# Two-layer hybrid backbone, attention stage: value halves side by side, neighbour bias added by TensorE, normaliser divided out by GpSimd

## The reference

```python
s = jnp.einsum('bqhd,bkhd->bhqk', q, k).astype(jnp.float32) * scale
p = jax.nn.softmax(s, axis=-1).astype(v.dtype)
return jnp.einsum('bhqk,bkhd->bqhd', p, v)
# B, latent queries: 8x16 window on a grid 64 wide, learned bias, then all context keys
s_loc = jnp.einsum('bwhd,brwkhd->bhwrk', qr, kn).astype(jnp.float32) * NA_SCALE
s_loc = (s_loc + bias.astype(jnp.float32)).reshape(B, H, GRID_W, kr * kc)
p = jax.nn.softmax(jnp.concatenate([s_loc, s_ctx], axis=-1), axis=-1).astype(v.dtype)
```

## Time and profile before

| | us |
|---|---|
| median of 3 runs | 3155.1 (3154.56 to 3157.39) |
| the profiled execution, its own time | 3152.75 |
| its span, first to last instruction | 3151.2 |
| TensorE busy (matmuls) | 3005.9 (95%) |
| VectorE busy | 1641.4 (52%) |
| ACT busy | 917.2 (29%) |
| GpSimd busy | 223.2 (7%) |

### The profile page before, as it was taken

The page is one execution under the profiler, slowest core; times in us unless marked ns, Lnnn a source line. Parts: engine busy times, 40 slices in busy tenths (PEclk is TensorE's granted clock), DMA queues, the critical chain, the costliest instruction groups (busy, mean ns, idle before and its releaser), DMA issues. The chain is left out here.

```text
span 3151.2 us, 44954 instructions
## 1 busy us (share of the span) xinstructions
PE 3005.9 (95%) x17054; PEld 2608.0 (83%) x17054; DVE 1641.4 (52%) x2910; ACT 917.2 (29%) x1433; POOL 223.2 (7%) x252
## 2 busy tenths in 40 slices
PE   7999999989988899999999899999998989999999
PEld 3888888878978787888888788888876979778887
DVE  4664466444466736652664566255244467643333
ACT  2221122123366522211222222112222367432221
POOL 1300000021213100000000000000002123000000
PEclk9999999999999999999999999999999999999999
DMA  7543243212100023332432234233212200223332
GB/s 240 124 126 100 80 126 106 81 53 56 44 13 1 26 61 104 112 112 65 127 116 85 67 113 134 59 111 100 72 50 67 66 12 7 67 80 106 88 96 91
DMA packets 412202, 263.55 MB, mean 84 GB/s; under 512 B 11700, under 2 KB 403672, under 8 KB 412088
## 3 DMA queue, kind: packets, MB, share of 16 engines
q1 hardware_dynamic: 407256, 253.14, 26.9%
q0 software_dynamic: 2752, 4.66, 0.9%
q10 hardware_dynamic: 2080, 4.19, 0.4%
HBM read 256.13 MB, written 6.68 MB: 83 GB/s over the span
## 5 line engine op out<-in xcount | busy, mean ns | idle before, releaser
L406 PE MATMUL pair<-h_hi,w_hi 128*128 128x512 f32 x2912 | 1029.9, 354 | 46.9 <-DVE h_lo L529 23.2
L407 PE MATMUL pair<-h_lo,w_hi 128*128 128x512 f32 x2912 | 963.4, 349 | 0.0
L410 PE MATMUL pair<-h_hi,w_lo 128*128 128x512 f32 x2912 | 819.9, 350 | 0.0
L406 PEld LDWEIGHTS pair<-h_hi,w_hi 128*128 128x128 f32 x2912 | 555.3, 191 | 181.6 <-issue 46.5
L407 PEld LDWEIGHTS pair<-h_lo,w_hi 128*128 128x128 f32 x2912 | 555.5, 191 | 73.3
L380 DVE TENSOR_TENSOR w_lo<-w_raw,w_hi 128x1024 fp32r<-128x1024 f32 (+1 forms) x276 | 362.7, 1315 | 307.5 <-ACT w_hi L373 301.0
L410 PEld LDWEIGHTS pair<-h_hi,w_lo 128*128 128x128 f32 x2912 | 471.8, 192 | 19.8
L373 ACT ACTIVATE w_hi<-w_raw 128x1024 fp32r<-128x1024 f32 (+1 forms) x276 | 307.8, 1116 | 614.1 <-PE pair L410 589.0
L406 PE MATMUL pair<-s_hi,w_hi 128*128 128x512 f32 x1232 | 426.6, 346 | 0.0
L407 PE MATMUL pair<-s_lo,w_hi 128*128 128x512 f32 x1232 | 400.5, 344 | 0.0
L647 DVE SCALAR_TENSOR_TENSOR mod_acc<-mod_raw,cs,mod_acc 128x256 f32<-128x256 f32 x896 | 365.3, 480 | 0.0
(11 more groups left out here) (215 smaller groups left out, 3390.7 us busy)
## 6 DMA issues: line engine op xcount, KB each, us to landing
mod_raw<-in_w_mod SPq DMA_DIRECT2D x64, 1024.0 KB, 5.0
w_raw<-in_w_ffn_gate SPq DMA_DIRECT2D x88, 512.0 KB, 3.8
w_raw<-in_w_ffn_up SPq DMA_DIRECT2D x88, 512.0 KB, 3.8
w_raw<-in_w_ffn_down SPq DMA_DIRECT2D x64, 704.0 KB, 4.6
w_raw<-in_w_in SPq DMA_DIRECT2D x32, 512.0 KB, 4.0
w_raw<-in_w_out SPq DMA_DIRECT2D x12, 512.0 KB, 4.1
w_raw<-in_w_q_up SPq DMA_DIRECT2D x8, 576.0 KB, 4.1
mod_first<-in_w_mod ACTq DMA_DIRECT2D x2, 2048.0 KB, 12.3
```

Of the source, the lines that this page charges most:

```text
L406: eng.matmul(dst, wh, rh, start=first, stop=False)
L407: eng.matmul(dst, wh, rl, start=False, stop=False)
L410: last = eng.matmul(dst, wl, rh, start=False, stop=end)
```

## The change

Four things change in the attention stage.

Values: `v_hi` and `v_lo` of one head lie side by side in one stationary operand of 128 columns (`v_both`, `vn_both`). One matmul with `p_hi` gives v_hi p_hi in rows 0 to 63 and v_lo p_hi in rows 64 to 127, and a second, of 64 columns, adds v_hi p_lo to the first half. The two halves are added when y is evicted. The values of the neighbour heads are split per pair instead of all at once.

Bias: the tables themselves are split into `na_hi` (ACT) and `na_lo` (VectorE), and TensorE adds them to the scores with two matmuls of a split identity. Maximum and exponential of all chunks read PSUM. `bias_at` gives the steps of the eight splits: 2 and 4 of each layer, 56 and 62 of layer 0, 38 and 42 of layer 1. `na_lo` takes the place of `na_tt` in memory.

Normaliser: ACT copies the spread reciprocals to `inv_sum`, one row buffer, and one half of y to `y_f`; VectorE adds the other half; GpSimd multiplies a whole head pair's y by `inv_sum` once it is complete (`pair_ends`, step 4 of the next pair). What waited for y (`y_hi`, the loads of the output weights) waits for `a_scaled`.

Start: ACT copies the identity to fp32r.

```diff
 TensorE
+    if biased(l, s):
+        eng.wait_ge(bias_lo_done, bias_tables(l, s))
     for a, b in keys:
         eng.matmul(dst, qh[rows, q], kh[rows, a:b], start=True, stop=False)
         eng.matmul(dst, qh[rows, q], kl[rows, a:b], start=False, stop=False)
+        if biased(l, s) and a == 0:
+            for table in (na_hi, na_lo):
+                eng.matmul(dst, ident_r[:, :], table[:, j, first:first + SEQ], start=False, stop=False)
...
+    vals = v_both[:, :, 2 * i + j, :] if kind == "mla" else vn_both[i][:, :, j, :]
-        eng.matmul(dst, vh[:, k, i * P:(i + 1) * P], ph, start=k == kc[0], stop=False)
-        eng.matmul(dst, vh[:, k, i * P:(i + 1) * P], pl, start=False, stop=False)
-        last = eng.matmul(dst, vl[:, k, i * P:(i + 1) * P], ph, start=False, stop=k == kc[-1])
+        if first:
+            eng.matmul(dst, vals[:, k, :], ph, start=True, stop=False)
+        last = eng.matmul(dst[0:V_DIM], vals[:, k, 0:V_DIM], pl, start=False, stop=False)
+        if not first:
+            last = eng.matmul(dst, vals[:, k, :], ph, start=False, stop=end)
 ACT, even step from 6 on, then after the exponential
     eng.wait_ge(a_pv, c0 // 2 + b + 1)
+    wait_if(eng, a_scaled, 6 * l + 2 * b // att_chunks(l))
+    eng.activation(inv_sum[r, q0:q0 + 2 * P], psum2[r, bank + 2 * P:bank + 4 * P], ACT.Copy).then_inc(a_inv, 1)
-    eng.activation(y_f[r, ...], psum2[r, bank:bank + 2 * P], ACT.Copy).then_inc(a_copied, 1)
+    eng.activation(y_f[r, ...], psum2[other, bank:bank + 2 * P], ACT.Copy).then_inc(a_copied, 1)
...
+    if bias_at(l, s):
+        i, j = bias_at(l, s)
+        eng.wait_ge(tt_loaded[j], 16 * (2 * l + i + 1))
+        eng.activation(na_hi[:, j, :], na_tt[:, j, :], ACT.Copy).then_inc(bias_hi_done, 1)
 GpSimd
+    k = pair_ends(l, s)
+    if k is not None:
+        eng.wait_ge(a_out, (ATT_C0[l] + (k + 1) * att_chunks(l)) // 2)
+        eng.tensor_tensor(y_f[:, k, 0:w], y_f[:, k, 0:w], inv_sum[:, 0:w], ALU.mult).then_inc(a_scaled, 1)
 VectorE, step s
     eng.wait_ge(a_s, c0 + s + 1)
-    if not own_scores(l, s):
-        eng.tensor_tensor(prob[:, s % 3, 0:SEQ], pair[s % 2][:, 0:SEQ], na_tt[:, j, first:first + SEQ], ALU.add)
-        eng.tensor_copy(prob[:, s % 3, SEQ:TOK], pair[s % 2][:, SEQ:TOK])
     eng.tensor_reduce(stat[:, s % STATS, 0:1], ..., AX_X, ALU.max, negate=True).then_inc(a_max, 1)
+    if bias_at(l, s):
+        i, j = bias_at(l, s)
+        eng.wait_ge(bias_hi_done, 4 * l + 2 * i + j + 1)
+        eng.tensor_tensor(na_lo[:, j, :], na_tt[:, j, :], na_hi[:, j, :].bitcast(F32), ALU.subtract)\
+           .then_inc(bias_lo_done, 1)
     (reciprocal of chunk s-1)
     (even step: y)
+    eng.wait_ge(a_inv, c0 // 2 + b + 1)
     eng.wait_ge(a_copied, c0 // 2 + b + 1)
-    eng.tensor_tensor(y, y, psum2[r, bank + 2 * P:bank + 4 * P], ALU.mult).then_inc(a_out, 1)
+    eng.tensor_tensor(y, y, psum2[r, bank:bank + 2 * P], ALU.add).then_inc(a_out, 1)
     (pt_lo of chunk s-2)
 SyncE, tables of the second neighbour pair
-    eng.wait_ge(a_max, ATT_C0[l] + 4 * nb + (nb // 2) * (j + 1))
+    eng.wait_ge(a_s, ATT_C0[l] + 4 * nb + (nb // 2) * j + SEQ // P)
```

More of the change, by code:

```diff
@@ L263, in program @@
         vn_f = sb("vn_f", [P, TOK // P, NA_WIDTH], F32, "sarea", na_at + 4 * TOK * 4)
-        v_hi = sb("v_hi", [P, TOK // P, MLA_HEADS * V_DIM], F32R, "sarea", 0)
-        v_lo = sb("v_lo", [P, TOK // P, MLA_HEADS * V_DIM], F32R, "sarea", 4 * TOK * 4)
+        v_both = sb("v_both", [P, TOK // P, MLA_HEADS, 2 * V_DIM], F32R, "sarea", 0)
         y_f = sb("y_f", [P, 6, TOK], F32, "harea", KD * TOK * 4)
-        vn_hi = sb("vn_hi", [P, TOK // P, NA_WIDTH], F32R, "sarea", 14 * TOK * 4)
-        vn_lo = sb("vn_lo", [P, TOK // P, NA_WIDTH], F32R, "sarea", na_at + 4 * TOK * 4)
+        vn_both = [sb(f"vn_both{i}", [P, TOK // P, 2, 2 * NA_DIM], F32R, at, off * TOK * 4)
+                   for i, (at, off) in enumerate((("harea", 4), ("sarea", 14)))]
         wo_first = sb("wo_first", [P, 2, KD * P], F32, "sarea", 8 * TOK * 4)
@@ L285, in program @@
                                    ("ks_lo1", "wring", 12)))]
+        ident_r = sb("ident_r", [P, P], F32R)
         na_tt = sb("na_tt", [P, 2, BIAS_SLOTS * GRID_W], F32, "scratch", 0)
+        na_lo = sb("na_lo", [P, 2, BIAS_SLOTS * GRID_W], F32R, "scratch", 0)
+        na_hi = sb("na_hi", [P, 2, BIAS_SLOTS * GRID_W], F32R, "wring", 13 * TOK * 4)
+        inv_sum = sb("inv_sum", [P, TOK], F32, "scratch", 3 * TOK * 4)
         mod_raw = sb("mod_raw", [P, KD, 2 * P], F32)
@@ L350, in program @@
         a_hi, a_lo, v_hi_done = sem("a_hi"), sem("a_lo"), sem("v_hi_done")
-        a_s, a_max, a_exp, a_rsum, a_copied, a_t, a_pth, a_ptl, a_pv, a_out, a_bias = (
-            sem(f"a_{k}") for k in ("s", "max", "exp", "rsum", "copied", "t", "pth", "ptl", "pv", "out", "bias"))
+        a_s, a_max, a_exp, a_rsum, a_copied, a_t, a_pth, a_ptl, a_pv, a_out = (
+            sem(f"a_{k}") for k in ("s", "max", "exp", "rsum", "copied", "t", "pth", "ptl", "pv", "out"))
+        a_inv, a_scaled = sem("a_inv"), sem("a_scaled")
+        bias_hi_done, bias_lo_done, ident_ready = sem("bias_hi_done"), sem("bias_lo_done"), sem("ident_ready")
         a_latent_t, a_latent_hi, a_latent_lo = (sem(f"a_latent_{k}") for k in ("t", "hi", "lo"))
@@ L1168, in mix_act @@
                         eng.wait_ge(c_read, C_READS * l + 3)
-                        eng.activation(token_values(v_hi, t), unit_values(o), ACT.Copy, scale=c_stat[:, 3, t:t + 1])\
+                        eng.activation(token_values(0, t), unit_values(o), ACT.Copy, scale=c_stat[:, 3, t:t + 1])\
                            .then_inc(v_hi_done, 1)
@@ L1485, in program @@
         ATT_C0 = [0, 6 * 12]
-        ATT_SPLITS = 21
+        ATT_SPLITS = 22
         def chunk_info(l, c):
@@ L1517, in splits, with biased, bias_tables, bias_at @@
             i = g - MLA_HEADS
[L1518 to L1523, removed]
-            kind, _, _, q0, _ = chunk_info(l, c)
-            return kind == "mla" or q0 >= SEQ
+            values = vn_f[:, :, i * P:(i + 1) * P].rearrange("p k (j d) -> p k j d", j=2)
+            return 2 * MLA_HEADS + 3 * i, [(na_f[:, i, 0:w], qh[:, 0:w], ql[:, 0:w]), (na_f[:, i + 2, :], kh[:, :], kl[:, :]),
+                                           (values, vn_both[i][:, :, :, 0:NA_DIM], vn_both[i][:, :, :, NA_DIM:])]
+        def biased(l, c):
+            kind, _, _, q0, _ = chunk_info(l, c)
+            return kind == "na" and q0 < SEQ
+        def bias_tables(l, c):
+            kind, i, j, _, _ = chunk_info(l, c)
+            return 4 * l + 2 * i + j + 1
+        def bias_at(l, s):
+            nb = att_chunks(l)
+            per = nb // 2
+            return {2: (0, 0), 4: (0, 1), 4 * nb + per + 2: (1, 0), 5 * nb + 2: (1, 1)}.get(s)
         def latent_parts(l, c):
@@ L1531, in latent_parts, with pair_ends @@
                        if chunk_info(layer, x)[3] < SEQ)
-        def bias_steps(l, c):
-            return sum(2 for layer in range(l + 1) for x in range(c if layer == l else n_chunks(layer))
-                       if not own_scores(layer, x))
+        def pair_ends(l, s):
+            nb = att_chunks(l)
+            return (s - 4) // nb - 1 if s > 4 and (s - 4) % nb == 0 else None
         Y_ORDER = [0, 1, 2, 3, 6, 7, 4, 5]
@@ L1681, in attention_pool @@
             split(0)
-            for s in range(n):
+            for s in range(n + 6):
+                k = pair_ends(l, s)
+                if k is not None:
+                    eng.wait_ge(a_out, (ATT_C0[l] + (k + 1) * att_chunks(l)) // 2)
+                    eng.tensor_tensor(y_f[:, k, 0:w], y_f[:, k, 0:w], inv_sum[:, 0:w], ALU.mult).then_inc(a_scaled, 1)
+                if s >= n:
+                    continue
                 g, new = att_group(l, s)
@@ L1871, in _ @@
                 first_mod_load(act, n)
+            act.wait_ge(const_loaded, 16)
+            act.activation(ident_r[:, :], ident[:, :], ACT.Copy).then_inc(ident_ready, 1)
             act.wait_ge(acc_free[0], 1)
```

48 lines of the change are left out of this document (20 added, 28 removed).

## The result

The changed kernel takes 3215.47 us (median of 4 runs, 3211.14 to 3217.53), beside 3154.83 for the kernel before in the same session: 1.92% slower, ratio 1.0192, 95% interval [1.0174, 1.0209]. The forecast of 3174 us had the direction right and the size wrong: +61 in place of +20.

The account below looks back on a forecast made before the run. TensorE was taken to bound the latent heads and VectorE the neighbour heads, by a thin margin. Terms 23.6 + 2.8 + 6 - 1.6 - 1.5 - 2.1 - 6.3 - 1.4 = +19.5 gave 3174 us, range 3157 to 3191.

Parts of the forecast that it names:

- Tables' split: Attention stages: eight waits for na_hi and na_lo in VectorE's in-order queue delay pt_lo and the next transposes, +23.6 us.
- Clock: Attention stages: eight new TensorE stalls lower its granted clock afterwards, 0 to 11 us, taken as +6.
- a stretch of 3.4 us at 1.2 GHz: After each stall: one short low-clock stretch, costing up to 1.7 us where TensorE limits, 1.1 in the opening steps.
- Neighbour heads' steps: Neighbour heads of both layers: steps get shorter, -2.1 us in layer 1 and -6.3 in layer 0.
- in the neighbour heads VectorE is the limit: Neighbour heads before the change: VectorE sets the pace, busy 44.51 of 46.86 us in layer 1, 3.35 a step.
- Latent heads: Latent heads: value matmuls saved against a longer y chain, -1.6 us in layer 1 and -1.5 in layer 0.
- six steps of twelve are TensorE's: Layer 0's latent heads: six of twelve steps are bound by TensorE and gain 0.36 us each.
- Ends: End of each attention stage: +2.8 us for copy and w_lo's wait on GpSimd, -0.7 a layer for fewer matmuls.
- The start: Before attention: the identity copy lies in the start's waits and costs 0.
- rival A: Attention: TensorE's backlog hides tables and longer chain, only its matmuls count, -22.4 us or 3133; chance 0.08.
- rival B: Attention: tables cost 23.6 us and ends 2.8, but TensorE's saving is felt in full, 3159; chance 0.14.
- Rival C: Attention: 0.6 us waits in every even step bring ten more low-clock stretches of 1.7 us, 3191; chance 0.12.

Follow-up runs that it names:

- kernel 1: Changed kernel with ACT making na_hi one step earlier and VectorE making na_lo behind pt_lo, so that neither stands in the chain: 3175.75 us.
- kernel 3: Changed kernel with the two bias matmuls ahead of the score matmuls instead of between them: 3192.62 us.
- kernel 4: Changed kernel with VectorE adding y behind pt_lo of its step instead of ahead of it: 3163.66 us.
- kernel 5: Changed kernel with the 64 bias matmuls left out, the tables still split and waited for: 3179.78 us, one run.
- Kernel 2: Changed kernel with the bias added by VectorE again, no tables split and no bias matmuls: 3158.39 us, ratio to before 1.0018.
- kernel 8: The kernel before the change, with VectorE multiplying y behind pt_lo instead of ahead of it: 3138.69 us, ratio to before 0.9946.
- kernel 6: Changed kernel with the edits of kernel 1, kernel 3 and kernel 4 together: 3124.78 us, ratio to before 0.9908.
- kernel 10: kernel 6 with ACT's two copies of an even step behind exp of that step instead of ahead of it: 3138.72 us.
- kernel 7: Changed kernel with the edits of Kernel 2 and kernel 4 together: 3122.72 us, ratio to before 0.9895.

## Why the prediction was right in sign and wrong in size

- **Tables' split, 23.6 us**: right, mechanism and size. The stalls measured 10.8 in the neighbour heads (forecast 13.2), and the openings grew by 10.6 (forecast 10.4).
- **Clock, 0 to 11 us, taken as 6**: wrong. In the neighbour heads alone kernel 1 gives back 15.5 us beyond the stalls, and two low stretches in layer 0's latent heads cost 0.9 (4.25 in place of 3.79, twice). The step that failed is "a stretch of 3.4 us at 1.2 GHz": I priced each stall with one short stretch, while here the clock stayed low for 23.9 us in a row with TensorE busy all the time. The stalls were the same in kernels 3, 4 and 5 within 0.6 us, with 13.7, 6.8 and 6.8 us low. Why the clock stayed low for so long in the changed kernel stays open.
- **Neighbour heads' steps, -8.4 us**: wrong, +10.5 (kernel 1 against before: 4.3 and 6.2). This is the largest failure, 19 us, and 22 with the 2.9 us of the next item. The step that failed is "in the neighbour heads VectorE is the limit". TensorE was busy for 46.86 of 46.86 us in the very row that I read the earlier trace rows, as it is in the latent heads. With that, its 0.47 a step for the bias less 0.36 could not vanish; and the 0.47 was 0.87, since two changes of the row count came with it. The rows before could have told both: latent and neighbour steps have nearly the same count of matmuls (186 in 8 and 324 in 14), and take 3.03 and 3.35. What differs is the two changes of rows in a neighbour step, from the values (128) to the scores (64) and on to the transposes (128); the latent scores have 96. In layer 0 the kernel before had 6.8 us of low clock in these heads and kernel 1 none, so that the 4.3 is rather too small than too large.
- **Latent heads, -3.1 us**: wrong, +7.5 (6.5 by kernel 1). 2.9 of it (1.4 and 1.5) is not the latent heads' own: it lies in the last three steps of each stretch, which hold the first biased scores (in layer 1 3.57, 4.07 and 3.60 in place of 3.06, 3.57 and 3.12). With 0.9 of low clock, 3.7 is left for the y chain, all of it in layer 0. Kernel 2, without bias matmuls, has 120.6 and 80.4 beside 117.1 and 80.7. In layer 1 the steps came near the forecast, 3.49 and 3.77 even, 2.44 odd; a pair takes 6.07 on the mean, where the forecast had 5.96 and the kernel before 6.06. The later copy is 0.47 for the odd head, over the end I gave. In layer 0 the step that failed is "six steps of twelve are TensorE's". Of the six odd steps four fell, by 0.28 or 0.34, and two, with context keys alone, stayed at 2.19: TensorE waited 0.6 us in them before, so they were already the chain's. Three even steps grew by 0.46 or 0.47, and the one with the next head's splits from 3.02 to 4.03. The twelve took 32.98 us before and 33.94 in kernel 1.
- **Ends, +1.4 net**: right, +1.6. w_lo took 1.84 and 2.38 us where it had 1.23, 1.8 more in all (forecast 2.2).
- **The start, 0**: +7.3 in this pair of profiles. 6.4 of it is a wait of VectorE for modulation weights between 100 and 145 us. That wait differs between executions: 3.5 us in the kernel before, 9.9 in the changed one, 1.7 in kernel 1, 8.0 in kernel 8, whose program is the one before up to attention. Kernels 1, 5 and 6 have the changed kernel's program up to attention and reach T(0) at 896.1 to 896.9 us, as the kernel before does (896.6); kernels 3, 4 and 10, with the same program there, reach it at 901.2 to 904.8. So the wait comes and goes without the change, and the profiled execution of the changed kernel caught it. Its other three executions have no trace.

By size, from +19.5 to +64.7, with the 2.9 and the 0.9 us put where they belong: neighbour steps +21.8, clock +10.4, start and rest +8.6, latent heads +6.8, less 2.4 for the stalls. The sign was right by the stalls, which came as forecast. The rest of the sum had the sign wrong: without the stalls and the clock it says -10.1, and kernel 1, which has neither, is 22 us above the kernel before (3175.8, 3153.5). TensorE's saving, which rivals A and B counted in full, is seen only once y and the tables are off the chain (kernels 6 and 7). Rival C was on the right side of the forecast, but what it priced at 17 us came to 0.9: the clock fell twice for 3.4 us in layer 0's latent heads, each time after a wait of 1.2 us. The long low stretches stood in the neighbour heads with their stalls.

## What to carry to other kernels

When two engines are both busy for a whole stretch, neither can be called the limit by its share: compare with a stretch that has the same instructions on one of them and ask what its extra time is, or take work off one of them and see whether the stretch shortens. Price a new matmul with its neighbours in the queue, since a stationary of another row count cost 0.2 us at each of its sides here. Put what others don't wait for (here y and the tables) behind what they do in an in-order queue, and look at what then stands behind its own wait.

## What the runs showed of the hardware that was not expected

- Each change between stationaries of 64 and 128 rows cost TensorE about 0.2 us at the full clock (kernels 3 and 6 against the changed kernel and kernel 1). In the latent heads, with 96 beside 128 rows, no load waits for its own matmul in this way (scores at 2651.12 follow a value product at 2651.01).
- In the changed kernel the granted clock stayed at 1.2 GHz for 23.9 us though TensorE had no gap in them; in kernels 3, 4 and 5, with the same stalls within 0.6 us, the longest low stretch there was 10.2, 6.8 and 3.4 us.
- The same waits of up to 1.4 us in layer 0's latent heads left the clock at 1.00 in kernel 1, and brought two low stretches of 3.4 us in the changed kernel.
- Two ACT copies of 64x256 start 0.40 us apart, while one followed by an exponential can take 0.26.
